# A three-layer transformer kernel on one core: state-space signs folded into the powers, first results later, norm roots in columns

## What is computed

```python
for l in range(2):                                     # first block
    shift, scale, gate = split(silu(c) @ w_ada[l] + b_ada[l])
    h = rms_norm(x, norm_g[l]) * (1 + scale) + shift
    u, z_s, q, k, v, z_a = split(h @ w_in[l])          # 2048 -> 6144
    y_s = s5_mixer(u, ...) * silu(z_s)                 # state space, 64 groups of 16, gelu, w_glu
    y_a = diff_attention(rope(q), rope(k), v, ...) * silu(z_a)
    x = x + gate * (concat(y_s, y_a) @ w_out[l])
x = rms_norm(x, final_g)
z = rms_norm(x, pre_mix) @ w_in2                       # second block: 2048 -> 68 tiles
mix = g_rw * (rwkv7(z) @ w_branch_rw) + g_mla * (mla(z) @ w_branch_mla)
x = x + rms_norm(mix @ w_out2, post_mix)
f = conv_gelu(rms_norm(x, pre_ffn) @ w_up) @ w_down    # 2048 -> 11264, 5632 -> 2048
x = x + rms_norm(f, post_ffn)
x = x + rms_norm(sigmoid(x @ w_pg) * (p @ w_ple), ple_norm)
```

## Time and profile before

| what | value |
|---|---|
| median of 3 runs | 3246.94 us (3246.91 to 3251.76) |
| profiled execution | 3253.76 us, span 3252.0 us |
| TensorE busy | 2995.8 us, 92% |
| VectorE busy | 2265.5 us, 70% |
| ScalarE busy | 1624.1 us, 50% |
| GpSimd busy | 334.0 us, 10% |
| chain that ended last | TensorE 59%, VectorE 25%, ScalarE 8%, DMA 4%, issue 3% |
| DMA | 577.01 MB, mean 177 GB/s |

### The profile page before, as it was taken

The page is one execution under the profiler, slowest core; times in us unless marked ns, Lnnn a source line. Parts: engine busy times, 40 slices in busy tenths (PEclk is TensorE's granted clock), DMA queues, the critical chain, the costliest instruction groups (busy, mean ns, idle before and its releaser), DMA issues.

```text
span 3252.0 us, 60643 instructions
## 1 busy us (share of the span) xinstructions
PE 2995.8 (92%) x24264; PEld 2768.1 (85%) x24264; DVE 2265.5 (70%) x3538; ACT 1624.1 (50%) x2409; POOL 334.0 (10%) x587
## 2 busy tenths in 40 slices
PE   6889989998988799999899999999799999999987
PEld 2677777887977789999798889989799999999987
DVE  6367777588788877775666566666688845887565
ACT  3335655355565554745334342545555544555454
POOL 0012322100123131300000000110100000000000
PEclk8899999998999899999999998999899999999989
DMA  9877766874645346555233333555355555555543
GB/s 372 290 241 239 242 207 214 282 276 138 184 134 155 103 151 204 177 175 171 91 102 106 101 112 100 166 159 187 127 172 184 183 188 177 185 184 169 187 145 115
DMA packets 168745, 577.01 MB, mean 177 GB/s; under 512 B 39760, under 2 KB 39792, under 8 KB 156048
## 3 DMA queue, kind: packets, MB, share of 16 engines
q1 hardware_dynamic: 146784, 525.40, 49.1%
q0 software_dynamic: 21104, 44.27, 4.6%
q10 hardware_dynamic: 576, 3.47, 0.3%
HBM read 546.83 MB, written 17.83 MB: 174 GB/s over the span
## 4 chain that ended last, share of the span: by engine, by line
PE 59%; DVE 25%; ACT 8%; DMA 4%; issue 3%; SPq 1%; DVEq 0%; ACTq 0%; POOL 0%
PE acc L950 58%; DVE arena L910 7%; DVE rounded L910 6%; ACT arena L947 4%; DVE arena L920 3%; ACT rounded L947 2%; DVE upper L910 2%; DVE upper L920 1%; ACT L947 1%; ACT upper L947 1%; DVE rounded L920 1%; PE acc L953 1%; SPq L906 1%; DMA arena<-in_w_ada 1%; DMA arena<-in_w_in 1%
## 5 line engine op out<-in xcount | busy, mean ns | idle before, releaser
L950 PE MATMUL acc<-rounded 128*128 128x256 f32 x14688 | 1941.2, 292 | 52.9 <-issue 30.3
L950 PEld LDWEIGHTS acc<-rounded 128*128 128x128 f32 x14688 | 1845.3, 196 | 137.8 <-issue 103.8
L910 DVE TENSOR_TENSOR rounded<-arena,rounded 128x1024 fp32r<-128x1024 f32 (+1 forms) x832 | 1003.9, 1207 | 311.7 <-ACT rounded L947 242.8
L947 ACT ACTIVATE rounded<-arena 128x1024 fp32r<-128x1024 f32 (+1 forms) x864 | 883.8, 1023 | 648.7 <-PE acc L950 449.1
L950 PEld LDWEIGHTS acc<-upper_rounded,rounded 128*128 128x128 f32 x4560 | 553.2, 193 | 25.8 <-issue 14.2
L950 PE MATMUL acc<-upper_rounded,rounded 128*128 128x256 f32 x4560 | 560.8, 285 | 9.6 <-DVE rounded L910 5.5
L947 ACT ACTIVATE arena<-arena 128x256 f32<-128x256 f32 (+4 forms) x477 | 252.9, 530 | 308.5 <-DVE arena L910 207.3
L950 PE MATMUL acc<-arena 128*32 128x512 f32 (+5 forms) x1622 | 250.3, 480 | 59.8 <-DVE arena L910 22.8
L910 DVE TENSOR_TENSOR arena<-arena 128x256 f32<-128x256 f32 (+5 forms) x471 | 258.6, 549 | 49.9 <-ACT arena L947 30.1
L910 DVE TENSOR_TENSOR arena<-acc,arena 128x256 f32<-128x256 f32 (+3 forms) x280 | 119.0, 425 | 204.0 <-PE acc L950 181.1
L920 DVE SCALAR_TENSOR_TENSOR arena<-arena 128x256 f32<-128x256 f32 (+5 forms) x461 | 205.6, 446 | 59.2 <-ACT arena L947 31.2
(11 more groups left out here) (91 smaller groups left out, 1194.3 us busy)
## 6 DMA issues: line engine op xcount, KB each, us to landing
arena<-in_w_in SPq DMA_DIRECT2D x328, 512.0 KB, 4.5
arena<-in_w_ada SPq DMA_DIRECT2D x88, 1024.0 KB, 5.2
arena<-in_w_up SPq DMA_DIRECT2D x176, 512.0 KB, 4.1
arena<-in_w_down SPq DMA_DIRECT2D x88, 512.0 KB, 4.1
arena<-in_w_outa SPq DMA_DIRECT2D x32, 512.0 KB, 6.0
arena<-in_w_glu SPq DMA_DIRECT2D x32, 512.0 KB, 6.2
arena<-in_w_outm SPq DMA_DIRECT2D x32, 512.0 KB, 4.6
arena<-in_w_out SPq DMA_DIRECT2D x32, 512.0 KB, 4.3
```

Of the source, the lines that this page charges most:

```text
L910: return self.put(self.e and self.e.tensor_tensor(o, a, b, op))
L947: return self.put(self.e and self.e.activation(o, a, f, scale=scale, **kw))
L950: return self.put(self.e and self.e.matmul(o, l, r, start=start, stop=stop, skip_group_check=True))
```

## The change

1. **Signs.** `P1` and `P2`, and `QR` and `QI`, are multiplied by `sgn` once a layer, in operations that become SCALAR_TENSOR_TENSOR. The 32 multiplications of the C factors in `s5_prep` go. In `PQ` the two signs cancel.
2. **First half of the results.** `s5_back` waits, for half 0, for tile 43 of 48 of w_in before it appends `s5_out`. Half 1 stays where it was.
3. **Roots in columns.** For the four tags above TensorE makes the sums with the squares as the stationary operand and one column of ones, two matmuls with one column each, so a token lies on a partition. ScalarE takes the root of 128 x 2 (`NCOL`), VectorE the reciprocal of 128 x 2, and TensorE spreads it over all partitions by two matmuls against the identity into PSUM bank 3. VectorE reads it from there in `h` and in the new `scale`.
4. **warm.** A root of one column is put on ScalarE at the first matmul of tile 15 of w_outm (both layers), w_out2 and w_down1.
5. **post** is cut into `scale` and `post`, ordered by `scaled`: scale of group g + 1 and nothing more stands ahead of the low parts of group g. The squares are summed on VectorE (`sum4`), one every 8 blocks of w_up.
6. **w_pg** leaves PAIRS: its first 64 blocks go four tiles by four k (`QUADS`), packed so on the host.
7. **Earlier work.** `LW` is loaded once the first tile of w_in2 is done. The tiles of p are split when the first half of tile 87 of w_up is done.

The diff, cut to its core (the allocation of `NCOL`, the tables of beats and the same edit of `QR` and `QI` are left out):

```diff
-PAIRS = (("w_in", 48), ("w_in2", 0), ("w_up", 0), ("w_pg", 0))
+PAIRS = (("w_in", 48), ("w_in2", 0), ("w_up", 0))
...
+QUADS = (("w_pg", 0),)
...
             n, k = n0 + at // nk, at % nk
-            if at % 16 == 0 and not ((name, u0) in PAIRS and blk < 16):
+            quads = (name, u0) in QUADS
+            if quads and blk < 64:
+                n, k = n0 + blk // 4 % 4, 4 * (blk // 16) + blk % 4
+            if at % 16 == 0 and not ((name, u0) in PAIRS and blk < 16) and not (quads and blk < 32):
                 self.want(name, u0 + at // 16)
             if blk % 8 == 0:
+                if (name, n, k) == ("w_up", 87, 8):
+                    self.spared = p
+                    for i in range(2):
+                        self.add("part", "p", i)
                 p = self.halves
...
             self.add("mm", t, k, p, blk % 8)
+            if (name, n, k) in (("w_outm", 15, 0), ("w_out2", 15, 0), ("w_down1", 15, 0)):
+                self.add("warm")
             if blk % 8 == 7:
...
                 held.append(t)
-            if late is not None and blk == 39:
+            if late is not None and blk == (71 if quads else 39):
                 late()
...
             for _ in range(8):
+                yield
+            while half == 0 and ("w_in", l, 43) not in self.marks:
                 yield
...
+    def scaled(self, tag, g):
...
+        if g == 0:
+            self.add("scale", tag, 0)
+        self.add("post", tag, g)
+        if g < 3:
+            self.add("scale", tag, g + 1)
...
+    def square_sums(self):
+        yield
+        for g in range(1, 4):
+            self.add("sum4", g)
+            yield
...
         self.add("recip", "mo")
-        for g in range(5):
-            if g < 4:
-                self.add("post", "mo", g)
-            if g:
-                for k in range(4 * g - 4, 4 * g):
-                    self.add("hf", k)
-                self.add("sqf", g - 1)
+        for g in range(4):
+            self.scaled("mo", g)
+            for k in range(4 * g, 4 * g + 4):
+                self.add("hf", k)
+            self.add("sqf", g)
         self.add("ff_first")
+        self.bgs.append(self.square_sums())
...
-        for k in range(2):
-            self.add("part", "p", k)
...
-        for g in range(5):
-            if g < 4:
-                self.add("post", "fo", g)
-            if g:
-                self.add("xs", g - 1)
+        for g in range(4):
+            self.scaled("fo", g)
+            self.add("xs", g)
...
+            self.add("scale", "em", g)
...
         pe.wait_ge("sum_dve", ("ev", tl.out_of[total[0], total[1], total[2]].o))
-        pe.mm(B(3, 0, 256), con("ones"), V(RS2, 256), True, True).then_inc("norm_pe", tag)
+        for th in range(2):
+            x = pe.mm(B(3, th, 1), V(RS2 + 128 * th, 128), con("ones", 1), True, True)
+        x.then_inc("norm_pe", tag)
...
+    def recip(tag):
+        if tag in ("x0", "hf"):
+            return
+        pe.wait_ge("norm_dve", ("col", tag))
+        for th in range(2):
+            x = pe.mm(B(3, 128 * th, 128), V(NCOL + th, (0, 128)), con("ident"), True, True)
+        x.then_inc("norm_pe", ("over", tag))
...
     def rmsf():
-        pe.wait_ge("sum_pool", ("hf", 3))
+        pe.wait_ge("sum_dve", ("hf", 3))
+        pe.wait_ge("x_dve", ("mo", 3))
         for i in range(4):
...
-                pe.wait_ge("norm_act", ("sqrt", ("x", 0) if l else "x0"))
+                if l:
+                    pe.wait_ge("rhs", ("h", 1, 15))
+                else:
+                    pe.wait_ge("norm_act", ("sqrt", "x0"))
...
     def rms(tag, total):
         act.wait_ge("norm_pe", tag)
-        act.act(V(RS, 256), B(3, 0, 256), ACT.Sqrt, bias=con("eps"), scale=1.0 / 2048).then_inc("norm_act", ("sqrt", tag))
+        if total is None:
+            to, sums = V(RS, 256), B(3, 0, 256)
+        else:
+            to, sums = V(NCOL, 2), B(3, 0, 2)
+        act.act(to, sums, ACT.Sqrt, bias=con("eps"), scale=1.0 / 2048).then_inc("norm_act", ("sqrt", tag))
...
+    def warm():
+        act.act(V(NCOL + 2, 1), con("eps"), ACT.Sqrt)
...
     def part(tag, j):
...
-        free = {"yr": ("w_in2", 0, 67), "ya": ("w_brw", 0, 15), "mx": ("w_bmla", 0, 15), "p": ("w_up", 0, 87),
+        free = {"yr": ("w_in2", 0, 67), "ya": ("w_brw", 0, 15), "mx": ("w_bmla", 0, 15),
...
-        if isinstance(tag, str) and (tag != "cq" or j >= 4):
+        if tag == "p":
+            act.wait_ge("mm", ("half", tl.spared))
+        elif isinstance(tag, str) and (tag != "cq" or j >= 4):
...
     def recip(tag):
         dve.wait_ge("norm_act", ("sqrt", tag))
-        dve.recip(V(RS, 256), V(RS, 256))
+        if tag in ("x0", "hf"):
+            dve.recip(V(RS, 256), V(RS, 256))
+        else:
+            dve.recip(V(NCOL, 2), V(NCOL, 2)).then_inc("norm_dve", ("col", tag))
...
         for j in ([k] if k % 4 == 0 and l == 0 or k == 0 else []) + ([k + 1] if k < last else []):
-            dve.stt(V(UT + 256 * j, 256), V(X + 256 * j, 256), V(GP + j, 1), V(RS, 256), MUL, MUL).then_inc("h_dve", (l, j))
+            if l:
+                dve.wait_ge("norm_pe", ("over", ("x", 0)))
+            root = B(3, 0, 256) if l else V(RS, 256)
+            dve.stt(V(UT + 256 * j, 256), V(X + 256 * j, 256), V(GP + j, 1), root, MUL, MUL).then_inc("h_dve", (l, j))
         dve.wait_ge("h_act", (l, k))
...
             dve.wait_ge("s5_act", ("p", l, 1))
-            dve.tt(V(P1, 576), V(P1, 576), V(PK, 576), MUL)
-            dve.tt(V(P2, 576), V(P2, 576), V(PK, 576), MUL)
+            for at in (P1, P2):
+                dve.stt(V(at, 576), V(at, 576), con("sgn"), V(PK, 576), MUL, MUL)
         if i == 7 and part == 0:
...
         def ch(base, n):
...
-        if i == 0:
+        if i == 1:
             dve.wait_ge(f"l_bc{b % 2}", (l, b))
-            dve.ts(V(BC + 128, 128), V(BC + 128, 128), con("sgn"), None, MUL)
-        if i == 1:
             if b:
...
+    def sum4(g):
+        dve.wait_ge("norm_act", ("sqf", g))
+        dve.tt(V(AR, 1024), V(AR, 1024), V(AR + 1024 * g, 1024), ADD).then_inc("sum_dve", ("hf", g))
...
+    def scale(tag, g):
+        src, stream, sem = {"mo": (MO, "w_out2", "ev_act"), "fo": (FO, "w_down1", "g_act"), "em": (EM, "w_pg", "g_act")}[tag]
+        t = V(src + 1024 * g, 4, 256)
+        dve.wait_ge(sem, ("ev", tl.out_of[stream, 0, 4 * g + 3].o))
+        dve.wait_ge("norm_pe", ("over", tag))
+        dve.tt(t, t, B(3, 0, (0, 4), (1, 256)), MUL)
...
     def post(tag, g):
-        src, stream, sem = {"mo": (MO, "w_out2", "ev_act"), "fo": (FO, "w_down1", "g_act"), "em": (EM, "w_pg", "g_act")}[tag]
-        t, x = V(src + 1024 * g, 4, 256), V(X + 1024 * g, 1024)
-        dve.wait_ge(sem, ("ev", tl.out_of[stream, 0, 4 * g + 3].o))
-        dve.tt(t, t, V(RS, (0, 4), (1, 256)), MUL)
+        src, x = {"mo": MO, "fo": FO, "em": EM}[tag], V(X + 1024 * g, 1024)
         dve.tt(x, x, V(src + 1024 * g, 1024), ADD).then_inc("x_dve", (tag, g))
...
-    def rw_first():
-        pool.wait_ge("rw_dve", "gd")
+    def rw_zero():
+        pool.wait_ge("mm", ("out", tl.out_of["w_in2", 0, 0].o))
         pool.dma(V(LW, 384), D["lora"][0], "l_lw", 0)
...
-    def sqf(g):
-        pool.wait_ge("norm_act", ("sqf", g))
-        if g:
-            if g > 1:
-                pool.wait_ge("sum_pool", ("hf", g - 1))
-            pool.tt(V(AR, 1024), V(AR, 1024), V(AR + 1024 * g, 1024), ADD).then_inc("sum_pool", ("hf", g))
...
+def pack_quads(W):
...
+    b = W[:, :512].reshape(4, 4, 128, 4, 128).transpose(0, 2, 3, 1, 4)
+    return np.concatenate([b.reshape(4, 128, 2048), pack(W[:, 512:])])
...
-    A["w_pg"] = pack(g["w_ple_gate_2"][0])
+    A["w_pg"] = pack_quads(g["w_ple_gate_2"][0])
```

More of the change, by code:

```diff
@@ L100 @@
 HALF = 1024
-N1, N2 = 25348, 11392
+N1, N2 = 25348, 11400
 NF = NS * 2 * HALF + 2 * 4096
@@ L2674, in arrange @@
     order = np.concatenate([n, np.stack([16 + n, 24 + n, 32 + n, 40 + n], 1).reshape(-1), 8 + n])
-    A["w_in"] = np.concatenate([pack(w.reshape(2048, 48, 128)[:, order].reshape(2048, 6144)) for w in g["w_in"]])
+    A["w_in"] = np.concatenate([pack(w.reshape(2048, 48, 128)[:, order].reshape(2048, 6144))
+                                for w in g["w_in"]])
     A["w_outm"] = np.concatenate([pack(w[:1024]) for w in g["w_out"]])
```

16 lines of the change are left out of this document (8 added, 8 removed).

## The result

| | before | after |
|---|---|---|
| median of 4 runs | 3249.35 us (3246.91 to 3256.39) | 3204.82 us (3199.57 to 3208.96) |
| ratio, 95% interval | | 0.9849 (0.9828 to 0.987) |
| profiled span | 3252.0 us | 3202.1 us |

The kernel is 1.5% faster. A second sitting of the same kernel beside the experiments gave 0.9838 (0.982 to 0.9855). The prediction was 3201 us, within 3186 to 3226. The span of the profiled execution fell by 49.9 us.

What follows compares the result with a forecast made beforehand. TensorE, busy 92% of the span, was taken as the bound, with VectorE binding two state-space stretches. The terms 5 + 19 - 3 + 0 - 1 + 8 + 4 + 0.8 + 7.5 + 6 = 46.3 us gave 3201 us, range 3186 to 3226.

Steps and rivals of the forecast that it cites:

- +8, +11 and -3: First half of the results moved behind tile 43: +8 us in layer 0, +11 in layer 1, -3 at the end of w_in.
- Split by layer: Saving forecast per layer: +8 +2 -1.5 us in layer 0, +11 +3 -1.5 -1 in layer 1.
- Tail, -3: Last four tiles of w_in, both layers: low parts queue behind the moved results, costing 3 us (ends 0 and -10).
- rival C: Slower: moved results alternate between VectorE and ScalarE at w_in's end and TensorE waits at handoffs; about 3284 us, chance 0.04.
- Signs, +5: State-space batches: half of the removed sign multiplications hold TensorE, +2 us in layer 0 and +3 in layer 1.
- Before layer 1, 0, and after it, -1: Boundaries around layer 1: cheaper reciprocal offset by an extra table load, net 0; after w_outm of layer 1 only the load, -1.
- `mo`, +8: Boundary after w_out2: TensorE's last wait for low parts ends 8 us earlier (ends 5 and 10).
- First matrices, +7.5: First small matrices: earlier `LW` load removes a 5.89 us wait and half the slow clock, +7.5 us (ends 5.4 and 9.4).
- p, +6: At w_ple: splitting p earlier removes a 4.52 us wait and slow matmuls behind it, +6 us (ends 4 and 7).
- rival B: Boundaries give half, since each has another wait behind it: 13 of 26.3 us lost, 3214 us, chance 0.13.
- `fo`, +4: Boundary after w_down1: TensorE starts some 3 us earlier and the 0.98 us wait before 84 matmuls goes, +4 (ends 2 and 6).
- `em`, +0.8: Last root, without warm: 1.4 us less for the reciprocal, 0.70 more for spreading, +0.8 us.

Runs made afterwards that it cites:

- second profile: Profile of the changed kernel, nothing altered, run a second time beside the experiments: 3202.77 us, ratio 0.9838 to the kernel before.
- tiles 47 and 39: Changed kernel with the first half of the results waiting for that tile of w_in instead of 43: 47 gave 3214.92 us (0.988), 39 gave 3223.21 us (0.9898).
- order of the posts: Changed kernel with scale and add of the next group again ahead of this group's low parts: 3825.77 us, one run at a lower clock.

## Why the prediction was right, and where not

- **What bounds the kernel.** Right. The two windows with the earlier trace rows short of TensorE were VectorE's, and moving VectorE's work out of them was the largest part: 17 to 20 us between the kernels with and without the wait, where +8, +11 and -3 were forecast, 16. That VectorE alone held the results' stretch, and not ScalarE's part in them too, is argued from the waits and the chain.
- **Split by layer.** Wrong: 14.2 us in layer 0 and 7.9 in layer 1, where 8.5 and 11.5 were forecast. I had given layer 0 less because of its transfers. The wait for tile 43 alone gives 11.7 us in layer 0 and 8.3 in layer 1, where 8 and 11 were forecast. By windows of the second profile TensorE gets 9 us more in 400 to 500 us at a DMA share of 0.79 and 0.69. So the transfers left room there. In layer 1 the waits for ScalarE and VectorE remain (16.3 us for ScalarE and 12.6 for VectorE in 940 to 1180 us). Why layer 1 gives less than layer 0 was not tried.
- **Tail, -3.** The mechanism of rival C was real and its price small at tile 43. At tiles 47 and 39 it shows: 10 to 20 us. The 3.23 us that I put to TensorE there was a wait of VectorE for ScalarE. The step that I didn't take was to look for who else waits in order in w_in's last tiles, attention, and who reads the results.
- **Signs, +5.** Oversized: 0 to 4 us by the ratios, nothing by the profiles. The half that I took for the share on TensorE's way had no row behind it. That gaps between the batches now hide 0.36 us each is likely, but no run shows it.
- **Before layer 1, 0, and after it, -1.** 1.1 us better, and no loss can be told. The loads in w_outm cost nothing that shows.
- **`mo`, +8.** 7.3, and 1.1 of it is lost at the norm of w_up, whose sums wait 0.88 us for VectorE (they come 6.65 us behind that last wait and no longer 5.60): the cover that I had named. Within it: 0.3 us are the early root, not 1.28, because a `lo` of VectorE covers the load; 4.1 us of the last low part are GpSimd's absence, 3.5 left at the norm; the order of the posts gives the first low part 1.3 us and the last nothing. 0.5 us of the 7.3 are the clock at the spreading, which was slow in the second profile.
- **First matrices, +7.5.** 9.2 (8.9 by the run that undid it). Undersized: wait and slow clock both came back in full, as in its own upper end of 9.4; the next limit that I had set against them didn't come.
- **p, +6.** The step that failed: "TensorE waits 4.52 us, and 79 matmuls take 11.56 where 79 x 0.114 are 9.0. Split earlier: +6". It gave 0.8 us at most. Right behind the wait stood another, for a PSUM bank that ScalarE empties only after w_up's last activations: 0.49 and 3.32 us in place of 4.52. And the 2.5 us that the 79 matmuls took too long were the slow clock behind the wait, 4.27 us at 0.50. The new wait brings it back, 2.46 us at 0.50 from where TensorE starts again. It is rival B's mechanism, at one boundary out of five.
- **`fo`, +4.** 3.3, in two rows; 0.7 of it is w_pg's order.
- **`em`, +0.8.** 0.6.

The sum was 46.3 and the medians moved by 44.5 (52 by the second sitting). It came out near by luck, because errors of both signs cancelled. Some -5 for p, -1 to -5 for the signs and -2.5 in `mo` and `fo` stand against +1 to +4 for the moved results, +1.7 for `LW` and +2 around layer 1, where nothing was lost. These errors alone would put the saving at 38 to 46 us. The ledger's 49.9 holds 5.2 us more in its first and sixth rows, which can't be told from chance, and some 1.5 us between the norm of w_up and w_down1 whose cause was not looked for.

The two rules of the Trainium skill that the prediction named: the early root begins at 2276.12, where its load of 1.28 us ends (2274.83), so there is no pause of some 1.4 us as in the Trainium skill, "ScalarE: Activation LUTs", section "What ACT_TABLE_LOAD costs". And the scale from PSUM takes 1.22 us (2281.82), the add from SBUF beside it (2283.07) the same, against the extra cycles of "VectorE: DVE Perf Modes" in the Trainium skill, section "The TRN2 errata — SBUF-src ops pay a fixed extra latency per instruction". The measurement decides in both.

## What to carry to other kernels

Work of an engine that is full should be moved to where it is not, but the place is set by two others: who waits in order behind it, and who reads it. Four tiles too early or too late lost all or most of the gain. When a wait in front of short tiles is removed, look at the next resource that these tiles use up, here the PSUM banks and the queue that empties them, before the wait is counted as gain. A load or root that an engine does early is worth only what no other engine's queued work covers.

## What the runs showed of the hardware

- GpSimd beside VectorE, both from SBUF: VectorE's add of 128 x 1024 took 3.28 us against 1.22 alone, longer than GpSimd's own 2.41 us (sums of squares back on GpSimd).
- One execution (order of the posts) had a granted clock of 0.65 to 0.75 in every window of 500 us, also where TensorE was busy all the time (3000 to 3500 us, 0.75), and took 3825.77 us, where the kernel before in the same sitting took 3251 to 3258 in seven runs. VectorE's and ScalarE's operations were as long as ever (1.22 and 1.06 us for 128 x 1024).
- The reciprocal of 128 x 2 takes 0.17 us and that of 128 x 256 1.75; the root 0.26 and 0.47.
- A wait of 5.8 us for a transfer costs 8.9 us: behind it the granted clock is 0.50, and the four matmuls take 1.22 us where they take 0.70 at 1.00.
- The slow clock decides over small steps too: the same four matmuls of the spreading took 0.71 us in one profile of the changed kernel and 1.22 in the other, and the first scale came 0.5 us later.
